# A hybrid decoder block on one core: the second gate tile ahead of the last turned y, pooled tiles emptied ahead of a weight split, and a mixing product that waits for its rows one by one

## The reference

```python
proj = h @ w_in[i]
z, xbc, dt_raw, u, gates = jnp.split(proj, split_at, axis=-1)
y_ssd = ssd_branch(z, xbc, dt_raw, ...)          # (512, 2048) normed y @ w_ssd_out -> (512, 1024)
y_pool = pool_branch(u, pool_w[i], pool_scale[i])
g_ssd, g_pool = jnp.split(jax.nn.sigmoid(gates), 2, axis=-1)
x = x + (g_ssd * y_ssd + g_pool * y_pool) @ w_mix_out[i]
h = rms_norm(x, ffn_norm_g[i])
x = x + moe_ffn(h, ...)                          # router, top 4 of 32 experts
```

## Time and profile before

| | |
|---|---|
| median of 3 runs | 1928.0 us (1927.64 to 1928.16) |
| the profiled execution's own time | 1927.23 us |
| its span in the profile | 1925.5 us |
| TensorE busy | 1833.7 us (95%) |
| VectorE, ScalarE, GpSimd busy | 1405.7, 1173.6, 338.6 us |
| granted TensorE clock, mean | 0.98 of full |

### The profile page before, as it was taken

The page is one execution under the profiler, slowest core; times in us unless marked ns, Lnnn a source line. Parts: engine busy times, 40 slices in busy tenths (PEclk is TensorE's granted clock), DMA queues, the critical chain, the costliest instruction groups (busy, mean ns, idle before and its releaser), DMA issues.

```text
span 1925.5 us, 25022 instructions
## 1 busy us (share of the span) xinstructions
PE 1833.7 (95%) x8925; PEld 1514.1 (79%) x8925; DVE 1405.7 (73%) x1007; ACT 1173.6 (61%) x921; POOL 338.6 (18%) x313
## 2 busy tenths in 40 slices
PE   6999999889998888999999999999999999999977
PEld 5878888667888756888888888888888888888866
DVE  3566776453234357889889889898898898898863
ACT  4555455232222246777777777777777777777754
POOL 5023334430000210211111112112111111111000
PEclk9999999899999889999999999999999999999989
DMA  5343343332336247999999999999999999999941
GB/s 160 107 121 99 110 120 99 96 123 87 89 121 272 75 156 280 369 364 369 372 371 370 364 380 367 369 379 370 367 375 374 365 374 367 378 361 370 373 160 44
DMA packets 153032, 503.96 MB, mean 262 GB/s; under 512 B 15373, under 2 KB 75445, under 8 KB 119348
## 3 DMA queue, kind: packets, MB, share of 16 engines
q1 hardware_dynamic: 140916, 478.10, 66.5%
q0 software_dynamic: 12016, 25.08, 5.5%
q10 hardware_dynamic: 48, 0.07, 0.0%
HBM read 493.80 MB, written 25.90 MB: 270 GB/s over the span
## 4 chain that ended last, share of the span: by engine, by line
PE 82%; DVE 5%; ACT 5%; issue 3%; POOL 3%; DMA 1%; SPq 0%; ACTq 0%; DVEq 0%; POOLq 0%
PE gu_ps L1964 24%; PE dn_ps L1979 12%; PE gu_ps L1968 12%; PE gu_ps L1731 6%; PE gu_ps L1733 6%; PE gu_ps L1732 6%; PE dn_ps L1985 6%; PE et_ps L1950 3%; PE gu_ps L1955 1%; PE gu_ps L2102 1%; ACT w_hi L867 1%; POOL win L773 1%; PE gu_ps L1750 1%; DVE w_lo L1258 1%; POOL dx L759 1%
## 5 line engine op out<-in xcount | busy, mean ns | idle before, releaser
L1584 DVE TENSOR_TENSOR split_l<-ring,split_h 128x2048 fp32r<-128x2048 f32 x384 | 868.4, 2288 | 123.5 <-ACT split_h L1130 121.8
L1130 ACT ACTIVATE split_h<-ring 128x2048 fp32r<-128x2048 f32 x384 | 726.8, 1917 | 173.5 <-PE gu_ps L1968 140.5
L1964 PE MATMUL gu_ps<-split_h,xgT_h 128*128 128x512 f32 x1024 | 285.1, 400 | 1.5 <-DVE xgT_l L1590 1.5
L1964 PE MATMUL gu_ps<-split_h,xgT_l 128*128 128x512 f32 x1024 | 274.9, 390 | 0.0
L1968 PE MATMUL gu_ps<-split_l,xgT_h 128*128 128x512 f32 x1024 | 274.1, 389 | 0.0
L1964 PEld LDWEIGHTS gu_ps<-split_h,xgT_l 128*128 128x128 f32 x1024 | 192.8, 188 | 40.8
L1964 PEld LDWEIGHTS gu_ps<-split_h,xgT_h 128*128 128x128 f32 x1024 | 190.8, 189 | 43.0 <-DVE xgT_l L1590 2.0
L1968 PEld LDWEIGHTS gu_ps<-split_l,xgT_h 128*128 128x128 f32 x1024 | 192.4, 188 | 40.4
L1258 DVE TENSOR_TENSOR w_lo<-w_raw,w_hi 128x2048 fp32r<-128x2048 f32 (+1 forms) x45 | 103.8, 2306 | 151.4 <-ACT w_hi L867 151.4
L786 POOL COPY icur<-slots 128x1 int32 (+1 forms) x32 | 51.4, 1608 | 725.8 <-PE et_ps L1950 725.8
L1979 PE MATMUL dn_ps<-split_h,actT_h 128*128 128x512 f32 x512 | 161.4, 397 | 5.0 <-issue 5.0
(11 more groups left out here) (299 smaller groups left out, 2560.0 us busy)
## 6 DMA issues: line engine op xcount, KB each, us to landing
ring<-in_w_gate_up SPq DMA_DIRECT2D x256, 1024.0 KB, 7.0
ring<-in_w_down SPq DMA_DIRECT2D x128, 1024.0 KB, 8.1
w_raw<-in_w_in SPq DMA_DIRECT2D x28, 1024.0 KB, 5.7
arow<-acum_rows POOLq DMA_DIRECT2D x16, 512.0 KB, 6.6
w_raw<-in_w_ssd_out SPq DMA_DIRECT2D x8, 1024.0 KB, 5.3
w_raw<-in_w_in SPq DMA_DIRECT2D x9, 512.0 KB, 6.3
w_raw<-in_w_mix_out SPq DMA_DIRECT2D x4, 1024.0 KB, 7.8
wpg<-in_w_ple_gate SPq DMA_DIRECT2D x2, 2048.0 KB, 14.7
```

Source lines behind the costliest of these rows:

```text
L1130: a.activation(split_h[s % SPLIT][:, :], ring[s % RING][:, :], ACT.Copy).then_inc(hi_done, 1)
L1584: v.tensor_tensor(split_l[s % SPLIT][:, :], ring[s % RING][:, :], split_h[s % SPLIT][:, :].bitcast(F32), ALU.subtract).then_inc(lo_done, 1)
L1964: t.matmul(gu_ps[:, b * 512:b * 512 + 512], x[:, k, :], split_h[s][:, b * 512:b * 512 + 512], start=False, stop=False)
```

## The change

Three edits, all in the stage of the gates and the mixing product.

First, on TensorE, in the round q = 0: GS(0,1) is made ahead of the turned y of the last group, not behind it. The order of the two banks does not change, because each tile keeps its number in `projection_order`.

Second, on ScalarE, in the round q = 0: the high part of the last group's y (`turned_y(3)`) now stands ahead of the sigmoid of GP(0,1), and the split of the weights of SO(0,1) stands behind the emptying of the two pooled tiles. In the rounds q = 1 to 3 the order is as before.

Third, in the mixing product: TensorE no longer waits for all 8 low parts of mT ahead of a half tile (`m_low` at KD = 8), but for block n at the first matmul that reads block n.

```diff
--- before.py
+++ after.py
@@ -1033,13 +1033,13 @@
                     turned_y(1)
                     turned_y(2)
                 gates("GP", q, 0)
-                gates("GP", q, 1)
                 if q == 0:
                     turned_y(3)
-                mix_high(MIXN[("SO", q, 1)])
+                gates("GP", q, 1)
                 if q == 0:
                     wait_proj(act, ("PO", GR - 1, 1))
                     pool_out(("PO", GR - 1, 1))
+                mix_high(MIXN[("SO", q, 1)])
                 if q < 3:
                     mix_high(MIXN[("GS", q + 1)])
                     merged_high(2 * q)
@@ -1728,6 +1728,8 @@
                 if i >= 2 and first:
                     pe.wait_ge(pfree[i % 2], i // 2)
                 for n, (sh, sl, mh, ml) in enumerate(parts):
+                    if key[0] == "MO":
+                        pe.wait_ge(m_low, n + 1)
                     o = t.matmul(pb(key)[:, cols], sh, mh, start=n == 0, stop=False)
                     o = t.matmul(pb(key)[:, cols], sh, ml, start=False, stop=False)
                     o = t.matmul(pb(key)[:, cols], sl, mh, start=False, stop=n == len(parts) - 1)
@@ -1851,11 +1853,12 @@
                     t.matmul(st_ps[:, :], b_tok[:, c, :], xdd[:, :], start=True, stop=True).then_inc(st_done, 1)
             for q in range(4):
                 project(("GS", q, 0))
+                project(("GS", q, 1))
                 if q == 0:
                     for cc in range(CH):
                         pe.wait_ge(yn_done, 4 * (GR - 1) + 1 + cc)
                         turned(("y", GR - 1, cc), [zs[(GR - 1) % 2][:, cc, j * P:j * P + P] for j in range(4)])
-                for key in (("GS", q, 1), ("GP", q, 0), ("GP", q, 1)):
+                for key in (("GP", q, 0), ("GP", q, 1)):
                     project(key)
                 if q == 0:
                     project(("PO", GR - 1, 0))
@@ -1877,7 +1880,6 @@
                         if c == CH - 1 and h == 1 and i == 1:
                             turned_x1(c, 0)
                         wh, wl = columns(("M", 2 * h + i), 0, 256)
-                        pe.wait_ge(m_low, KD)
                         tile3(("MO", c, h), [(mT_h[:, k, ts], mT_l[:, k, ts], wh[:, k, :], wl[:, k, :]) for k in range(KD)],
                               slice(256 * i, 256 * i + 256), i == 0, i == 1)
```

## The result

The changed kernel takes 1916.8 us (median of four executions, 1912.14 to 1917.28); the kernel before, beside it on the same chip, 1927.8 us (1927.08 to 1928.16). The ratio is 0.9935, with a 95% interval of 0.9921 to 0.9949. The forecast was 1917.9 us. The profiled execution took 1916.7 us with a span of 1914.9 us, 10.6 us less than that of before.

The account below looks back on a forecast made before the run. The prediction took TensorE, with 82% of the last-ending chain, to bound the kernel. Turned y 5.4, pooled tiles 0.7 and mixing product 4.0 sum to 10.1 us, from 1927.2 to 1917.1, plus 0.8 for the median: 1917.9 us, range 1915.2 to 1921.5.

Parts of the forecast that it names:

- What bounds it: Whole kernel: TensorE holds 82% of the last-ending chain, so a microsecond counts almost only where TensorE waits.
- TensorE's three holes: Waits of 3.5 us for the turned y, 1.5 us ahead of SO(0,0), 2.9 us ahead of the first mixing matmul.
- The turned y: Round q = 0: GP(0,0) starts 5.4 us earlier, 3.5 from the hole, 1.9 from half clock and shorter copy waits.
- Who else must keep up: ScalarE's and VectorE's queues and the earlier SO(0,1) weight load cost nothing, with 2.9 us of cover.
- The pooled tiles: Ahead of SO(0,0): ScalarE is idle when they finish, saving 0.7 us; this edit alone would have gained nothing.
- The mixing product: Its start: 21 matmuls run in the hole, 28th starts 4.0 us earlier, 2.5 from work and 1.5 from clock.
- The added waits: Mixing product: the 112 added waits cost nothing; 21 us in all if each showed the whole weight load.
- The sum: Whole kernel: 5.4 + 0.7 + 4.0 = 10.1 us gained, giving 1917.9 us.
- rival 1: All 16 half tiles of the mixing product: the added waits show, 1939 us at 0.19 us each; 6 in 100.
- rival 2: Half clock falls elsewhere, among mixing matmuls or behind the turned y: 1916 to 1920 us; 20 in 100.
- rival 3: Cover used up at SO(0,0), or mixing product waits for something else; half the gain, 1921 to 1924 us; 7 in 100.
- rival 4: Behind the mixing product a transfer ends at a fixed time, so nothing comes through: 1928 us; 3 in 100.

Follow-up runs that it names:

- the first four experiments: Against the kernel before: only TensorE's order, only ScalarE's order, only the mixing product's waits, the first two edits together; 1921.8, 1924.4, 1923.0, 1920.5 us.
- the later logits: Changed kernel with the router's logits of chunks 0 and 1 each put behind one more half mixing tile; 1907.1 us, repeated 1910.0 us.
- the version with all edits: Changed kernel with both the leftover holes filled and the router's logits put later; 1909.2 us, repeated 1909.8 us.
- the last holes' edit: Changed kernel with pooled tiles emptied one by one and the first mixing tile's blocks 0 to 6 of both halves ahead of block 7; 1914.2 us.

## Why the prediction was right, step by step

**What bounds it.** TensorE's three holes were the right places, and the hole that the table called "issue" was a wait for `m_low`. "What is gained in the first round is carried through" held: 152.18 and 152.19 us from SO(0,0) to the end of SO(3,1).

**The turned y, 5.4 us.** Measured 5.29 (30.10 to 24.81 us from GS(0,0) to the pooled tiles), 5.26 by the first edit alone. GP(0,0) starts at 419.07, and the changed kernel's GS(0,0) came 0.39 us earlier, so 419.46 by before's clock; the forecast was 419.45. The theory that the hole would be filled by work that was ready anyway stands, and the windows show the clock's half of it: 1.00 at 417 to 420 us for 0.50.

**Who else must keep up, nothing.** Held. The low parts of y ended at 431.05 (forecast: near 431.9, the same five operations), 3.5 us ahead of need, and no wait for `yT_l` shows in any kernel that has the first edit.

**The pooled tiles, 0.7 us.** Measured 0.66. Wrong was the sentence that "this edit alone would have gained nothing". ScalarE's two moves without the first edit gained 0.65 us at the same place. The last low part of y was late in the kernel before because its high part was, and the change moves that up as well (it is one of the two moves). The emptying alone, without the high part, was not tried.

**The mixing product, 4.0 us.** Measured 4.01, and 4.00 as the only edit. The row of the 22nd matmul reads 0.39 us of idle time, but it starts 0.67 us behind the 21st (589.32 to 589.99), 0.55 more than a turn of 0.12; the forecast had 0.6. The 28th follows it 0.81 us later (589.99 to 590.80), as forecast. But of the term's two parts only 2.5 us, the work, is a firm price. That the 1.5 us of clock matched was luck in part: the profiled execution of before happened to lie in the middle of what such holes cost (0 in one kernel, 2.7 in another). The forecast should have put this spread into the term itself.

**The added waits, nothing.** Measured nothing, with 384 waits in place of 128. The Trainium skill ("TensorE: Matmul & The Clock Gate", step-by-step) says that weight loads are pulled ahead of running matmuls; a pitch of 0.12 us with weight loads of 0.19 us agrees, and the waits do not hinder it.

**The sum, 10.1 us.** 9.96 us at the three places, 0.39 from code ahead of the change, 0.37 on the way to the experts, 0.11 back: 10.6. The 0.39 and 0.37 have nothing to do with the forecast's mechanisms. One of the four executions, at 1912.14, was below the low end of 1915.2. The range was made from the mechanisms of the change and had no room for the spread between executions, which is larger than it seemed from three: the kernel before lay between 1922.4 and 1931.6 us in the 32 executions beside the first four experiments.

**The rivals.** The waits do not show (rival 1). The clock falls elsewhere (rival 2): not behind the turned y, which ran at 1.00, though TensorE did little but transposes from 416.55 to 419.07 us, as it had at 322 us at full clock. The Trainium skill ("TensorE: Matmul & The Clock Gate", PE-mode transpose) says that transposes do not count as busy for the clock gate in the way that other matmuls do. By that, the prediction said, a stretch of half clock (1.5 us) would come; neither of the two places shows one. Within the mixing product the stretches shifted, but the sum from the 49th to the last matmul came out as 61.36 us in both kernels. Of the seven other traces with the logits and the mixing tiles in the same order, five had 61.25 to 61.37 there and two 59.73 and 57.96, so this part of the rival was real and fell on zero. No cover was used up (rival 3), and no transfer held the end (rival 4): from the first expert matmul on, all kernels take 1219.6 to 1220.9 us.

## What to carry to other kernels

When an engine waits for the last of several pieces, let it start on the first: waits that are satisfied cost nothing here, however dense, so the only question is whether the next instruction in line has its data. Compare two traces by distances between the same events, not by totals: here, wherever the clock is the same, most of them repeat to 0.1 us, while the totals of one kernel spread by 9 us. Take the clock that a filled hole gives back as a range from zero: the same hole cost 0 to 2.7 us of it. And look at stretches of half clock in the middle of dense small matmuls, for they can be worth more than the holes: the later logits won 6.5 us of clock beside 5.1 us of idle time in the mixing product, and 7 to 11 us in the total, for two small products put off.

## What the runs showed of the hardware that I had not expected

- Executions differ before any edit is reached. GS(0,0) starts between 404.1 and 407.4 us in the fourteen traces, though the code ahead of it is the same. The windows from 96 to 104 us of the kernel before and of TensorE's order alone lie in the same code and have another clock:

```profile
96.00:104.00 8.00, 5.91 (x39) 4.91 (x38) 3.43 (x2) 6.48 (x9) 1.48 (x2) 1.00 0.45 131
```

```profile
96.00:104.00 8.00, 6.12 (x35) 5.28 (x34) 3.43 (x2) 6.04 (x8) 1.01 (x1) 0.79 0.45 131
```

- The same idle 2.94 us, ahead of the same matmuls, cost 0, 1.5, 1.5 and 2.7 us of clock in four kernels. What decides is open.
- No trace with work in the place of the hole has half clock there (none of ten ahead of the mixing product, none of eleven at the turned y), while of the traces with the hole three of four and three of three have it.
- The clock fell near 634 us in the version with all edits and not in the one without the last holes' edit, twice each, to the same 0.01 us of the product's length.
